# Seven products instead of eight for the last tile pair of the up projection

## The reference, cut to what matters

```python
h2 = _rmsnorm(x, g_ffn)
f = jnp.einsum("btd,df->btf", h2, w_up)            # 1024 -> 2 * 2816
f_gate, f_up = jnp.split(f, [D_FF], axis=-1)
f_conv, new_f = _causal_dwconv(f_gate, buf_f, conv_f_w)   # 3 taps
x = x + jnp.einsum("btf,fd->btd", jax.nn.silu(f_conv) * f_up, w_down)
```

## Time and profile before

| what | value |
|---|---|
| median of 3 runs | 836.84 us |
| time of the profiled execution | 836.67 us |
| its span | 834.9 us |
| TensorE busy | 825.1 us, 99% |
| VectorE busy | 713.9 us, 86% |
| ScalarE busy | 449.7 us, 54% |
| GpSimd busy | 165.5 us, 20% |
| mean granted clock of TensorE | 0.999 |

### The profile page before, as it was taken

One profiled execution on the slowest core, in us unless ns is written; L12 is line 12 of the kernel. 1 busy time (PEld: TensorE's weight loads), 2 busy tenths in 40 slices (PEclk: granted clock), 3 DMA queues, 4 the chain that ended last, 5 costly groups with the idle time before them and its releaser, 6 DMA issues.

```text
span 834.9 us, 18079 instructions
## 1 busy us (share of the span) xinstructions
PE 825.1 (99%) x6836; PEld 822.1 (98%) x6836; DVE 713.9 (86%) x1072; ACT 449.7 (54%) x814; POOL 165.5 (20%) x138
## 2 busy tenths in 40 slices
PE   8999999999999999999999999999999999999996
PEld 7999999999999999999999999999999999999996
DVE  6899898989999976766569899999999998967775
ACT  7753636454333234665236576667766666533553
POOL 2283737566000000000002210000000002500000
PEclk9999999999999999999999999999999999999999
DMA  9424223442342342235933116555554554335663
GB/s 264 128 79 117 84 83 93 134 118 88 101 116 83 100 113 76 84 94 70 202 107 102 50 45 171 127 127 127 132 134 115 140 126 136 99 87 116 138 139 106
DMA packets 191614, 95.02 MB, mean 114 GB/s; under 512 B 34552, under 2 KB 187020, under 8 KB 191524
## 3 DMA queue, kind: packets, MB, share of 16 engines
q1 hardware_dynamic: 183921, 86.02, 38.7%
q0 software_dynamic: 3456, 6.29, 4.4%
q10 hardware_dynamic: 4171, 1.82, 0.8%
HBM read 83.79 MB, written 3.51 MB: 105 GB/s over the span
## 4 chain that ended last, share of the span: by engine, by line
PE 94%; DVE 3%; issue 1%; DMA 1%; ACT 0%; SPq 0%; DVEq 0%; ACTq 0%
PE psum L2133 36%; PE psum L2139 18%; PE psum L2303 17%; PE psum L2308 9%; PE psum L2436 6%; PE psum L2442 3%; PE psum L2331 2%; PE psum L2336 1%; DMA raw<-in_w_in 1%; PE psum L2508 1%; PE psum L2176 1%; PE psum L2183 0%; PE psum L2174 0%; DVE w_lo L1623 0%; PE psum L2525 0%
## 5 line engine op out<-in xcount | busy, mean ns | idle before, releaser
L2133 PE MATMUL psum<-act,w_hi 128*128 128x260 f32 x1984 | 258.6, 283 | 0.0
L2133 PEld LDWEIGHTS psum<-act,w_hi 128*128 128x128 f32 x1984 | 246.3, 188 | 0.0
L2139 PE MATMUL psum<-act,w_lo 128*128 128x260 f32 x992 | 139.9, 283 | 0.0
L1317 DVE TENSOR_TENSOR w_lo<-raw,w_hi 128x1024 fp32r<-128x1024 f32 x78 | 103.1, 1323 | 34.8 <-ACT w_hi L718 34.5
L2139 PEld LDWEIGHTS psum<-act,w_lo 128*128 128x128 f32 x992 | 128.0, 188 | 0.0
L647 POOL TENSOR_TENSOR gate_a<-gate_a,prods 128x512 f32<-128x512 f32 x72 | 108.8, 1512 | 81.4 <-ACT prods L797 73.3
L2303 PE MATMUL psum<-act,w_hi 128*128 128x260 f32 x768 | 121.4, 282 | 0.0
L2303 PEld LDWEIGHTS psum<-act,w_hi 128*128 128x128 f32 x768 | 105.6, 188 | 0.0
L1623 DVE TENSOR_TENSOR w_lo<-raw,w_hi 128x1024 fp32r<-128x1024 f32 (+1 forms) x68 | 81.8, 1203 | 15.6 <-ACT w_hi L985 15.6
L718 ACT ACTIVATE w_hi<-raw 128x1024 fp32r<-128x1024 f32 x78 | 81.9, 1053 | 21.0 <-PE psum L2139 16.7
L985 ACT ACTIVATE w_hi<-raw 128x1024 fp32r<-128x1024 f32 (+1 forms) x68 | 69.6, 1030 | 37.0 <-PE psum L2308 23.9
(11 more groups left out here) (272 smaller groups left out, 1312.7 us busy)
## 6 DMA issues: line engine op xcount, KB each, us to landing
raw<-in_w_in SPq DMA_DIRECT2D x56, 512.0 KB, 3.7
raw<-in_w_up SPq DMA_DIRECT2D x44, 512.0 KB, 4.2
raw<-in_w_down SPq DMA_DIRECT2D x16, 448.0 KB, 3.9
w_lo<-raw POOLq DMA_DIRECT2D x24, 256.0 KB, 3.3
v<-in_x_prompt SPq DMA_DIRECT2D x8, 512.0 KB, 7.5
raw<-in_w_b_out SPq DMA_DIRECT2D x8, 512.0 KB, 4.0
raw<-in_w_a_out SPq DMA_DIRECT2D x8, 512.0 KB, 5.9
raw<-in_w_o SPq DMA_DIRECT2D x8, 512.0 KB, 4.3
```

The lines of the kernel that those rows point to most:

```text
L1317: ve.tensor_tensor(w_lo[:, slot, 0:k, :], raw[:, s, 0:k, :], w_hi[:, slot, 0:k, :], ALU.subtract).then_inc(lo_done, 1)
L2133: pe.matmul(a[:, h, :], w_hi[:, s, j, :], rhs(k, part)[:, h * H:(h + 1) * H], start=start and part == 0, stop=False)
L2139: last = pe.matmul(a[:, h, :], w_lo[:, s, j, :], rhs(k, 0)[:, h * H:(h + 1) * H], start=False, stop=stop)
```

## The change

Pair 21 leaves the table `PLAIN`, so that only pair 0 is plain. Pair 21 then runs as P1(21), P4(20), P2, P6, P5, P7, P3 of 21, and P4(21) is done inside job 22, ahead of its fourth contraction tile. Its partial results lie in PSUM bank 0 (`BANK_X`) and banks 6 and 7. Since pair 20 and pair 21 now follow each other as in the run, step 20 is the ordinary step of the run: VectorE forms the four weight sums for pair 21 in it. On ScalarE and VectorE the splits of token tiles 5 to 13 (`up_hi`, `up_lo`) are spread anew between the steps of pair 21. Job 22 now waits for token tile 20, and job 23 waits for token tile 21 where it waited for the gate half of pair 21.

```diff
-    PLAIN = (0, 21)
+    PLAIN = (0,)
...
-        BANK_GATE = {0: 0, 21: 0}
+        BANK_GATE = {0: 0}
...
         def hi_step(n):
-            if n >= FT - 1:
+            if n >= FT:
                 return down_step(n)
...
         def lo_step(n):
-            if n >= FT - 1:
+            if n >= FT:
                 return tuple(key for key in down_step(n) if key[0] != "4")
...
                 if j == KH - 1:
-                    pool.wait_ge(p_done, PRODUCT["up", FT - 1])
+                    pool.wait_ge(p_done, PRODUCT["P3", FT - 1])
...
                 if j == 0:
-                    pool.wait_ge(p_done, PRODUCT["up", FT - 1])
+                    pool.wait_ge(p_done, PRODUCT["P3", FT - 1])
...
+            def up_hi_after(name, first, last):
+
+                sc.wait_ge(p_done, PRODUCT[name, FT - 1])
+                for i in range(first, last):
+                    up_hi(i)
...
+            hi_4(FT - 1)
+            up_1(FT - 1)
             conv_first(FT - 2)
-            for i in range(EARLY_HI, EARLY_HI + 2):
-                up_hi(i)
-            hi_up(FT - 1)
+            hi_3(FT - 1)
+            hi_open(FT)
             silu(FT - 2)
-            for i in range(EARLY_HI + 2, EARLY_HI + 6):
-                up_hi(i)
-            hi_open(FT)
+            up_v(FT - 1)
+            up_hi_after("P6", EARLY_HI, EARLY_HI + 2)
+            up_5(FT - 1)
+            up_hi_after("P6", EARLY_HI + 2, EARLY_HI + KH)
+            up_hi_after("P5", EARLY_HI + KH, EARLY_HI + 2 * KH - 1)
             conv_first(FT - 1)
-            for i in range(EARLY_HI + 6, EARLY_HI + 8):
-                up_hi(i)
+            up_hi_after("P5", EARLY_HI + 2 * KH - 1, EARLY_HI + 2 * KH)
+            up_hi_after("P7", EARLY_HI + 2 * KH, KD)
+            hi_up(FT)
             silu(FT - 1)
-            for i in range(EARLY_HI + 8, KD):
-                up_hi(i)
-            hi_up(FT)
...
             up_gate(FT - 2)
+            lo_2(FT - 1)
             conv_rest(FT - 2)
+            lo_3(FT - 1)
+            lo_open(FT)
             up_product(FT - 2)
-            lo_up(FT - 1)
-            for i in range(EARLY_HI, EARLY_HI + 4):
-                up_lo(i)
-            plain_gate(FT - 1)
-            lo_open(FT)
+            up_los(EARLY_HI, EARLY_HI + 2)
+            up_22(FT - 1)
+            up_los(EARLY_HI + 2, EARLY_HI + 4)
+            up_gate(FT - 1)
+            up_los(EARLY_HI + 4, EARLY_HI + 6)
             conv_rest(FT - 1)
-            for i in range(EARLY_HI + 4, EARLY_HI + 6):
-                up_lo(i)
-            plain_product(FT - 1)
-            for i in range(EARLY_HI + 6, KD):
-                up_lo(i)
+            up_los(EARLY_HI + 6, EARLY_HI + 7)
+            up_product(FT - 1)
+            up_los(EARLY_HI + 7, KD)
             lo_up(FT)
...
+            pe.wait_ge(prod_done, START + 2 * KT + FT - 1)
             down_plain(0)
             turn_tail_f()
-            pe.wait_ge(cx_set, FT)
+            pe.wait_ge(prod_done, START + 2 * KT + FT)
             down_plain(1)
```

More of the change, by code:

```diff
@@ L391, in build @@
         assert not any(FOLLOWS[FT:]) and not SEVEN[-1]
-        assert PLAIN[0] == 0 and PLAIN[-1] == FT - 1 and SEVEN[1]
-        BANK_X = {1: 2, 2: 3, 3: 0, 4: 1, 5: 2, 6: 3, 7: 0, 8: 1, 9: 2, 10: 3, 11: 0, 12: 1, 13: 2, 14: 3, 15: 0, 16: 1, 17: 2, 18: 3, 19: 2, 20: 3}
-        BANK_GATE = {0: 0, 21: 0}
+        assert PLAIN == (0,)
+        BANK_X = {1: 2, 2: 3, 3: 0, 4: 1, 5: 2, 6: 3, 7: 0, 8: 1, 9: 2, 10: 3, 11: 0, 12: 1, 13: 2, 14: 3, 15: 0, 16: 1, 17: 2, 18: 3, 19: 2, 20: 3, 21: 0}
+        BANK_GATE = {0: 0}
         assert len(BANK_X) + len(BANK_GATE) == FT
@@ L1180, in _ @@
                     step_at_end_of_run(n)
+            hi_4(FT - 1)
+            up_1(FT - 1)
             conv_first(FT - 2)
-            for i in range(EARLY_HI, EARLY_HI + 2):
-                up_hi(i)
-            hi_up(FT - 1)
+            hi_3(FT - 1)
+            hi_open(FT)
             silu(FT - 2)
-            for i in range(EARLY_HI + 2, EARLY_HI + 6):
-                up_hi(i)
-            hi_open(FT)
+            up_v(FT - 1)
[3 more added lines that the diff above has]
+            up_hi_after("P5", EARLY_HI + KH, EARLY_HI + 2 * KH - 1)
             conv_first(FT - 1)
-            for i in range(EARLY_HI + 6, EARLY_HI + 8):
-                up_hi(i)
+            up_hi_after("P5", EARLY_HI + 2 * KH - 1, EARLY_HI + 2 * KH)
+            up_hi_after("P7", EARLY_HI + 2 * KH, KD)
+            hi_up(FT)
             silu(FT - 1)
-            for i in range(EARLY_HI + 8, KD):
-                up_hi(i)
-            hi_up(FT)
-            sc.wait_ge(p_done, PRODUCT["up", FT - 1])
+            sc.wait_ge(p_done, PRODUCT["P3", FT - 1])
             sc.dma_start(gf_row[:, :], g_final.rearrange("(o d) -> o d", o=1).broadcast_to([P, D])).then_inc(gf_in, 16)
@@ L1888, in _, with up_los @@
                     step_at_end_of_run(n)
+            def up_los(first, last):
+                for i in range(first, last):
+                    up_lo(i)
             up_gate(FT - 2)
+            lo_2(FT - 1)
             conv_rest(FT - 2)
+            lo_3(FT - 1)
+            lo_open(FT)
             up_product(FT - 2)
-            lo_up(FT - 1)
-            for i in range(EARLY_HI, EARLY_HI + 4):
-                up_lo(i)
-            plain_gate(FT - 1)
-            lo_open(FT)
-            conv_rest(FT - 1)
-            for i in range(EARLY_HI + 4, EARLY_HI + 6):
-                up_lo(i)
-            plain_product(FT - 1)
-            for i in range(EARLY_HI + 6, KD):
-                up_lo(i)
+            up_los(EARLY_HI, EARLY_HI + 2)
[3 more added lines that the diff above has]
+            up_los(EARLY_HI + 4, EARLY_HI + 6)
+            conv_rest(FT - 1)
+            up_los(EARLY_HI + 6, EARLY_HI + 7)
+            up_product(FT - 1)
+            up_los(EARLY_HI + 7, KD)
             lo_up(FT)
```

## The result

| what | before | after |
|---|---|---|
| median | 836.94 us (6 runs, 836.33 to 837.72) | 842.05 us (6 runs, 841.44 to 843.81) |
| ratio, 95% interval | | 1.0059, 1.0048 to 1.007 |
| time of the profiled execution | 836.67 us | 843.81 us |
| its span | 834.9 us | 842.0 us |
| mean granted clock of TensorE in it | 0.999 | 0.994 |

The kernel is 0.59% slower. The sign was forecast, the size was not: 842.05 us lies above the range of 837.0 to 840.7.

The account below looks back on a forecast made before the run. PE was taken to bound the kernel (busy 825.1 of 834.9 us). PE's gain of 1.38 us against 4.05 us of waiting for DVE gave +2.7 us: 839.5 us, 0.32% slower, range 837.0 to 840.7.

Parts of the forecast that it names:

- gain of PE: Pair 21 to job 22: job 22 reached 2.82 us earlier, P4(21) inside it costs 1.44, net gain 1.38 us.
- second half of job 22 starts: PE in job 22: reached at 703.01, first half with P4(21) takes 6.46 us, so second half starts at 709.47.
- three sums pushed by the DMA: Pair 21's DMA pushes three POOL down sums among `conv_rest(20)`, `lo_3`, `lo_open(22)`, costing DVE 1.40 us.
- fourth sum beside a split of a token tile: POOL's fourth down sum, released at 703.2, meets DVE's split of token tile 8 and costs DVE 0.55 us.
- `up_gate(21)` starts: DVE behind P3(21): 702.75 plus 1.95 us lost to POOL gives 704.70, 1.7 us behind P3(21).
- from there to the end of `lo_up(22)`: DVE's block for job 22: 7.64 us without POOL plus 3.85 us for POOL, ending at 716.19.
- PE's low pass starts: Job 22's low-weight matmuls start at 716.39, 0.2 us behind `lo_up(22)`, 4.05 us later than PE asks at 712.34.
- sum, from P1(21) to job 23: Net change: -1.38 us gained by PE plus 4.05 us of waiting, +2.7 us.
- PE's three stops: Second half of job 22, before token tiles 11 (about 0.8), 12 (about 1.0) and low weights (about 2.2): 4.05 us, released by DVE.
- the turns: DVE instructions with two SBUF inputs alternate with POOL's sums, 0.55 us each; about seven behind `up_gate(21)`, 3.85 us.
- the second rival: Convolution's instructions escape POOL, or only four to five turns fall behind `up_gate(21)`: +0.6 us, 837.4 us; chance 0.10.
- The clock falls in the stops: Job 22: a stop brings 1.2 GHz, 18 matmuls behind the last stop take twice as long, 841.7 us; chance 0.03.

Follow-up runs that it names:

- both repairs: Changed kernel with POOL's fourth and later sums waiting for `lo_up(22)`, and DVE and ScalarE splitting weights of jobs 22 to 24 earlier: 835.67 us, ratio 0.9988.
- the stops filled: Changed kernel with 5, 6 and 16 idle matmuls ahead of job 22's three waits (token tiles 11, 12, low weights): 840.54 us, ratio 1.0039.
- the DMA moved: Changed kernel with pair 21's DMA issued by POOL behind the three down sums of group 0 instead of ahead: 841.58 us, ratio 1.0061.

## Why the prediction was right or wrong

| step | forecast | measured |
|---|---|---|
| gain of PE | 1.38 us | stretch 1.23 and 1.36 us shorter where nothing stops (POOL held; both repairs) |
| second half of job 22 starts | 709.47 | 709.49 on the old scale |
| three sums pushed by the DMA | 1.40 us | 1.46 us |
| fourth sum beside a split of a token tile | 0.55 us | 0 |
| `up_gate(21)` starts | 704.70 | 704.36 |
| from there to the end of `lo_up(22)` | 11.49 us | 11.95 us |
| PE's low pass starts | 716.39 | 716.37 |
| clock | stays | falls, 1.64 us (1.53 without the 0.1 of the restart) |
| sum, from P1(21) to job 23 | +2.67 us | +4.29 us |

**Right: who is late, where and why.** PE's three stops stand where they were said to stand and with the releasers named. With POOL held back DVE needs 7.83 us for the block that was laid out at 7.64, and 11.95 with POOL, so the turns cost 4.1 us, where seven were counted for 3.85. `up_gate(21)` was 0.34 us earlier than forecast, since the fourth sum cost DVE nothing, the block was 0.46 us longer, and PE started 0.06 us behind `lo_up(22)` where a signal of 0.2 was assumed; the three errors cancel, so the 0.02 us between 716.39 and 716.37 is luck, though each term was near. The convolution's two instructions do take turns, in both tiles, against the second rival's row of 0.18. Nothing at P4(21), at the start of job 22 or 23, or on ScalarE stopped PE.

**The step that failed: the chance of the rival "The clock falls in the stops", and the argument against it.** The mechanism was listed, with a price of 2.15 us; it is 1.64, since the low clock came only at about 719.5, 0.3 us behind the restart, and was gone at 722.9, 0.3 us ahead of job 23. But it got 0.03, and by the times it is what happened in every run of the changed kernel: none is below 841.44, and with the stops filled none of four is above 840.72. The argument was "my longest stop is 2.2 us, half the idle stretch of the earlier trace rows". That took one stretch in which the clock is known to be low (4.9 us without a matmul) as if its length told what lowers it. A closer look at the end of the same trace would even have seemed to bear it out: the last matmul ends at 828.8, and the granted clock stays at 1.00 until about 832.5, 3.7 us later. But job 22 is another case. There three stops follow each other with some 0.7 us of matmuls between them, and no row of the kernel before has such a group; with the DMA moved the clock fell within a stop of 1.96 us. The argument looked at the longest stop alone, where the runs show that its length does not decide. With no row on a group of stops, 0.03 was too sure, and the top of the range should have gone to the rival's price, 841.7. The result is the sum of the forecast's own +2.67 and the clock: 4.31, against 4.29 in the trace.

**What is left of the difference.** From job 23 to the end of the span both kernels take 118.8 us (842.0 - 723.23 and 834.9 - 716.11), so the 4.29 us are all that the change did in the traces. The medians differ by 5.11 us. The other 0.8 us was not pinned down. Of the six runs of the changed kernel two lie near 841.45, with a mean clock of 0.996; that is 4.3 us above the kernel before in the later rounds (837.13 to 837.16), as in the traces. Three lie at 842.0 to 842.2 with 0.992 to 0.993. A low clock that lasts longer there would fit: in the profile with the DMA moved (mean clock 0.993) the way from the low pass to the low pass of job 23 takes 723.62 - 715.63 = 7.99 us, here 726.19 - 719.20 = 6.99. But no trace of such a run of the changed kernel was taken.

**Against the Trainium skill.** The rows show that most turns cost DVE 0.4 to 0.55 us, and the two of `conv_rest(20)` 0.73 each, beside sums that POOL records at 0.75 and 0.77 us when nothing holds them up. The Trainium skill, "SBUF — State Buffer", "Who interferes with whom", has the shared port held for the whole instruction; here that is the upper end, and most turns cost less. For the clock the filled stops show that TensorE keeps 2.4 GHz when the stops hold matmuls: 1.00 in both stretches from 716 to 724, and 0.94, then 0.64 without them. The Trainium skill, "TensorE: Matmul & The Clock Gate", Part 1, calls the slow clock the default that activity lifts, and the filled stops agree with it. That rule allowed the rival, but by itself it does not say how short a stop is enough, so it did not settle its chance.

## What to carry to other kernels

Before taking work from the engine that bounds, follow the engine that feeds it to the next deadline, with the helper that shares its port: here 12 matmuls fewer (1.4 us) cost four times that (4.05 and 1.64 us) because VectorE's pieces moved into GpSimd's sums, and holding GpSimd back by one semaphore plus an order that splits the next job's weights first turned +0.59% into -0.12 to -0.17%. Cost a group of short stops of TensorE at their length plus the low clock behind them, some 1.2 to 1.6 us here (a stop's price is its idle time and some 0.24 us more); if a stop can't be taken away, matmuls without use in it can keep the clock. Whoever holds work back has to look one job further: held alone, the same sums stopped PE in job 23.
